# A two-layer decoder trunk on one Trainium2 core: an up tile cast and the first output rows moved to GpSimd, filler products on TensorE, and three casts and sums in another order

## What is computed

```
def rms_norm(x, w):
    y = xf * lax.rsqrt(jnp.mean(xf * xf, axis=-1, keepdims=True) + EPS)
    return (y * w).astype(x.dtype)
def swiglu(h, w_gate, w_up, w_down):
    return (jax.nn.silu(h @ w_gate) * (h @ w_up)) @ w_down
...
for l in range(DEPTH):
    x = x + 0.5 * swiglu(rms_norm(x, ffn1_norm[l]), ffn1_w_gate[l], ffn1_w_up[l], ffn1_w_down[l])
    ...
    x = x + 0.5 * swiglu(rms_norm(x, ffn2_norm[l]), ffn2_w_gate[l], ffn2_w_up[l], ffn2_w_down[l])
return rms_norm(x, final_norm)
```

## Time and profile before

| | |
|---|---|
| median of 3 runs | 1041.63 us (1041.61 to 1042.81) |
| profiled execution, its own time | 1040.92 us |
| its span | 1039.1 us |
| mean granted TensorE clock | 0.997 |
| TensorE busy | 1024.7 us (99%) |
| VectorE, ScalarE, GpSimd busy | 741.5, 606.9, 212.3 us |

### The profile page before, as it was taken

One profiled execution on the slowest core, in us unless ns is written; L12 is line 12 of the kernel. 1 busy time (PEld: TensorE's weight loads), 2 busy tenths in 40 slices (PEclk: granted clock), 3 DMA queues, 4 the chain that ended last, 5 costly groups with the idle time before them and its releaser, 6 DMA issues.

```text
span 1039.1 us, 18922 instructions
## 1 busy us (share of the span) xinstructions
PE 1024.7 (99%) x6464; PEld 886.3 (85%) x6464; DVE 741.5 (71%) x1201; ACT 606.9 (58%) x1070; POOL 212.3 (20%) x253
## 2 busy tenths in 40 slices
PE   7999999999999999999999999999999999999997
PEld 6888888899987888888888888889989888888885
DVE  5777666799776766666686666668986876666665
ACT  6555555787555655555675555558774556555554
POOL 3755111100400221111122111110014003111111
PEclk9999999999999999999999999999999999999999
DMA  8866666585124576666647666665731238666661
GB/s 260 263 190 188 188 185 191 143 240 154 62 62 122 163 211 192 183 188 195 183 133 217 194 183 183 193 172 161 223 102 63 82 101 245 200 183 188 192 185 41
DMA packets 249882, 176.79 MB, mean 170 GB/s; under 512 B 5876, under 2 KB 235401, under 8 KB 249705
## 3 DMA queue, kind: packets, MB, share of 16 engines
q1 hardware_dynamic: 248800, 174.35, 56.7%
q0 software_dynamic: 400, 1.43, 0.4%
q10 hardware_dynamic: 632, 0.34, 0.1%
HBM read 175.05 MB, written 1.05 MB: 169 GB/s over the span
## 4 chain that ended last, share of the span: by engine, by line
PE 94%; DVE 2%; ACT 1%; POOL 1%; issue 1%; DVEq 0%; POOLq 0%; ACTq 0%
PE bank L737 29%; PE bank L740 15%; PE bank L721 13%; PE bank L722 13%; PE bank L723 13%; PE bank L746 1%; PE bank L781 1%; PE bank L1109 1%; PE bank L1122 1%; DVE xr L2044 1%; PE bank L1042 1%; PE bank L995 1%; DVE Wl L1828 0%; PE bank L788 0%; PE bank L1024 0%
## 5 line engine op out<-in xcount | busy, mean ns | idle before, releaser
L1828 DVE TENSOR_TENSOR Wl<-raw,Wh 128x1024 fp32r<-128x1024 f32 x324 | 417.9, 1298 | 78.7 <-ACT Wh L1374 78.6
L1374 ACT ACTIVATE Wh<-raw 128x1024 fp32r<-128x1024 f32 x324 | 331.7, 1054 | 82.8 <-PE bank L723 82.2
L737 PE MATMUL bank<-X,Wh 128*128 128x512 f32 x1344 | 336.8, 393 | 0.0
L737 PEld LDWEIGHTS bank<-X,Wh 128*128 128x128 f32 x1344 | 246.7, 188 | 49.0
L740 PEld LDWEIGHTS bank<-X,Wl 128*128 128x128 f32 x1344 | 182.8, 189 | 14.7 <-DVE Wl L1828 0.9
L616 POOL TENSOR_TENSOR gact<-gact,pooled 128x256 f32<-128x256 f32 x88 | 77.6, 882 | 569.5 <-DVE gact L1922 432.4
L740 PE MATMUL bank<-X,Wl 128*128 128x256 f32 x1344 | 187.4, 282 | 0.0
L721 PE MATMUL bank<-Wh,aH 128*128 128x512 f32 x336 | 132.8, 395 | 1.4 <-DVE aL L1943 1.3
L722 PE MATMUL bank<-Wl,aH 128*128 128x512 f32 x336 | 131.8, 392 | 0.0
L723 PE MATMUL bank<-Wh,aL 128*128 128x512 f32 x336 | 131.5, 392 | 0.0
L1480 ACT ACTIVATE dec<-bank 128x256 f32<-128x256 f32 x88 | 33.6, 382 | 125.0 <-PE bank L740 124.9
(11 more groups left out here) (308 smaller groups left out, 1290.2 us busy)
## 6 DMA issues: line engine op xcount, KB each, us to landing
raw<-in_ffn_w_gate SPq DMA_DIRECT2D x88, 512.0 KB, 4.0
raw<-in_ffn_w_up SPq DMA_DIRECT2D x88, 512.0 KB, 3.7
raw<-in_ffn_w_down SPq DMA_DIRECT2D x88, 512.0 KB, 4.4
raw<-in_w_in SPq DMA_DIRECT2D x48, 512.0 KB, 4.6
raw<-in_w_out SPq DMA_DIRECT2D x16, 512.0 KB, 3.3
cst<-in_consts POOLq DMA_DIRECT2D x1, 1200.0 KB, 8.4
xr<-in_x SPq DMA_DIRECT2D x2, 512.0 KB, 4.3
out_x<-big SPq DMA_DIRECT2D x3, 256.0 KB, 2.1
```

Source lines behind the costliest of these rows:

```text
L737: nc.tensor.matmul(b[:, :], piece(Wh, s)[:, k, :], X[:, k, :, :], start=k == 0, stop=False)
L1374: return nc.scalar.activation(Wh[:, s, 0:D_MODEL], raw[:, s, :], ACT.Copy).then_inc(hi_cast.sem, 1)
L1828: return nc.vector.tensor_tensor(Wl[:, s, 0:D_MODEL], raw[:, s, :], Wh[:, s, 0:D_MODEL].bitcast(F32), ALU.subtract).then_inc(lo_cast.sem, 1)
```

## The change

In the head GpSimd casts piece 1 (the up tile of tile 0) in place of ScalarE, which only passes the count on. TensorE multiplies the unit matrix five more times (`KEEP`) between its transposes and the first gate product. On ScalarE the cast of piece 4 moves behind the gate and up sums of tile 0. On VectorE the two `variance` sums stand ahead of the low cast of piece 1. In the tail GpSimd weighs token half 0 (two products of 128x512) and later scales it (two more), VectorE no longer weighs the second quarter of half 1 apart, and SyncE's order of output DMAs becomes (0,0), (0,1), (1,1).

```diff
+KEEP = 5
...
+            for b in range(2):
+                sp.wait_ge(out_pool.sem, 2 + b + 1)
+                sp.dma_start(out[0, 0:P, b * NW:(b + 1) * NW], big[:, 0, b * NW:(b + 1) * NW]).then_inc(out_written.sem, 16)
             sp.wait_ge(out_dve.sem, 1)
-            sp.dma_start(out[0, 0:P, 0:NW], big[:, 0, 0:NW]).then_inc(out_written.sem, 16)
-            sp.wait_ge(out_dve.sem, 2)
             sp.dma_start(out[0, P:SEQ, NW:], big[:, 1, NW:]).then_inc(out_written.sem, 16)
-            sp.wait_ge(out_dve.sem, 3)
-            sp.dma_start(out[0, 0:P, NW:], big[:, 0, NW:]).then_inc(out_written.sem, 16)
...
+            pool.wait_ge(landed[1].sem, 16)
+            nc.gpsimd.tensor_copy(Wh[:, 1, 0:D_MODEL], raw[:, 1, :]).then_inc(up_first.sem, 1)
             pool.wait_ge(*lo_cast.at(0, 2))
...
+            pool.wait_ge(norm_w_in.sem, 16)
+            for b in range(2):
+                o, r, w = row_half(b)      # big[:, 0, q], xr[:, 0, q], norm_w[:, q]
+                pool.wait_ge(*x_new.at(DEPTH, b + 1))
+                nc.gpsimd.tensor_tensor(o, r, w, ALU.mult).then_inc(out_pool.sem, 1)
+            pool.wait_ge(root_dve.sem, 1)
+            pool.wait_ge(out_pool.sem, 2)
+            for b in range(2):
+                o, r, w = row_half(b)
+                nc.gpsimd.tensor_scalar(o, o, stat[:, 0, 7:8], None, ALU.mult).then_inc(out_pool.sem, 1)
...
+            def keep_warm(n):
+                for _ in range(n):
+                    nc.tensor.matmul(bank[3][:, 0:2 * P], ident, cst[:, C_IDENT:C_FIRST], start=True, stop=True)
...
-                    for _ in range(WARM):
-                        nc.tensor.matmul(bank[7][:, 0:2 * P], ident, cst[:, C_IDENT:C_FIRST], start=True, stop=True)
+                    keep_warm(WARM)
                     for c, b in ROW_ORDER:
...
+                    keep_warm(KEEP)
                     first_pair(layer, f, None)
...
                 if first:
-                    hi_first(layer, 0, 1)
+                    act.wait_ge(up_first.sem, 1)
+                    act.wait_ge(*hi_cast.at(layer, 1))
+                    act.sem_inc(hi_cast.sem, 1)
...
                     hi_first(layer, 0, 3)
-                    hi_first(layer, 0, 4)
...
                 gate_low(layer, f, 0, 0)
                 up_low(layer, f, 0, 0)
+                if layer == 0 and f == 0:
+                    hi_first(layer, f, 4)
                 hi_first(layer, f, 2)
...
                     lo_piece(layer, 0, 0)
-                    lo_piece(layer, 1, 1)
                     for c in range(HALVES):
                         variance(layer, n, c)
+                    lo_piece(layer, 1, 1)
...
             last(1, 0)
             variance(DEPTH, 0, 0)
             dve.wait_ge(norm_w_in.sem, 16)
-            weigh(0)
+            dve.wait_ge(*x_new.at(DEPTH, 3))
+            nc.vector.tensor_tensor(big[:, 1, 0:NW], xr[:, 1, 0:NW], norm_w[:, 0:NW], ALU.mult).then_inc(weighed.sem, 1)
             last(1, 1)
             final_root(0)
-            weigh(1)
             variance(DEPTH, 0, 1)
-            finish_row(0)
             final_root(1)
-            dve.wait_ge(weighed.sem, 2)
-            nc.vector.tensor_scalar(big[:, 1, NW:], big[:, 1, NW:], stat[:, 1, 7:8], None, ALU.mult).then_inc(out_dve.sem, 1)
-            finish_row(1)
+            dve.wait_ge(*x_new.at(DEPTH, 4))
+            nc.vector.scalar_tensor_tensor(big[:, 1, NW:], xr[:, 1, NW:], stat[:, 1, 7:8], norm_w[:, NW:], ALU.mult,
+                                           ALU.mult).then_inc(out_dve.sem, 1)
```

More of the change, by code:

```diff
@@ L306, in build @@
         rows_in = signal("rows_in")
+        up_first = signal("up_first")
+        out_pool = signal("out_pool")
         small_in = signal("small_in")
@@ L692, in _, with row_half @@
                 ffn(layer, 1)
+            def row_half(b):
+                q = slice(b * NW, (b + 1) * NW)
+                return big[:, 0, q], xr[:, 0, q], norm_w[:, q]
+            pool.wait_ge(norm_w_in.sem, 16)
[8 more added lines that the diff above has]
+                nc.gpsimd.tensor_scalar(o, o, stat[:, 0, 7:8], None, ALU.mult).then_inc(out_pool.sem, 1)
         @block.tensor
@@ L2357, in _ @@
             last = update(DEPTH - 1, 2, 0.5, downs_done.at(DEPTH - 1, 2 * TILES))
[L2359 to L2363, removed]
             def final_root(c):
@@ L2369, in final_root @@
                 dve.wait_ge(root_dve.sem, c + 1)
[L2371 to L2375, removed]
             last(0, 0)
```

## The result

The changed kernel took 1044.34 us, the median of 20 executions (1043.24 to 1044.73); the kernel before took 1042.64 (20 executions on the same chip, 1041.42 to 1043.74). Ratio 1.0016 [1.0009, 1.0022]: 1.7 us more, small but outside the interval. I had 1041.4 with a range to 1043.4, and an effect of -0.2.

A forecast was written before the change was run, and what follows sets the result against it. GpSimd's DMA-issue queue bounds the head; behind TensorE's last product a mainly VectorE chain bounds the tail. Head -0.39 and tail +0.2 gave -0.2: 1041.63 - 0.2 = 1041.4 us, range 1040.2 to 1043.4.

The forecast's parts named there:

- A: The forecast itself: head and tail both near level, clock 1.00 behind the second wait, 1041.4 us; chance 0.42.
- B: Clock falls behind the longer wait before the first down product, in front of unbroken work: 1.57 us lost, 1043.0; chance 0.3.
- GpSimd's queue bounds the head: Head: GpSimd's unbroken DMA issues delay its scaling of tile 0, hence the first down product; issues shift by 0.25 us.
- the chain: Head, up to the first down product: scaling of tile 0 ends 0.39 us earlier, so 25.37 becomes 24.98.
- The filler: Head, TensorE: ten instructions in 2.3 us before the gate products; if the clock holds, wide products save 1.2 us.
- the second wait: Head, TensorE before the first down product of tile 0: grows to 1.95 us from 1.15, swallowing gains ahead of it.
- GpSimd's product holds VectorE's weighing: Tail: VectorE's weighing of (1,0) waits for GpSimd's second weighing, stretched to 1.5 us; the update behind it 0.8 late.
- GpSimd's two scalings of 0.64 each by the earlier trace: Tail: GpSimd scales token half 0 until 1034.85 us; if twice as long, the tail loses 0.7 more.
- the root's small step: Tail, VectorE: first step of the second root waits for GpSimd's scalings until 1034.85 us, 0.25 later.
- C: Tail: GpSimd doesn't hold VectorE, so the work taken off pays in full, 0.8 us earlier, 1040.4; chance 0.15.
- D: Head: the filler does not hold the clock, 0.50 again from 11.4 us; the wait covers it, 1041.4; chance 0.08.
- E: GpSimd's queue gets much faster, or the loops gain in some unseen way: under 1039.5 us; chance 0.05.

The follow-up runs named there:

- head_only: The changed kernel with the tail of the kernel before: 1042.86 us against 1042.64 for the kernel before, ratio 1.0002.
- head_pool: head_only with GpSimd's two scalings of tile 0 moved ahead of its DMA issues of gate columns and masks: 1039.46 us against 1042.26 for the kernel before.
- head_lowfirst: head_only with VectorE's low cast of piece 1 ahead of the two sums again: 1043.45 us against 1042.54 for the kernel before, ratio 1.0005.
- best: The changed kernel with GpSimd's tile 0 scalings ahead of its large DMA issues, and in the tail GpSimd weighing only quarter (0,0): 1038.90 us, ratio 0.9968 to before.
- best_keep0: best without the filler (KEEP = 0): 1039.91 us against 1042.36 for the kernel before, ratio 0.9975.
- tail_only: The kernel before with the change's tail alone: 1043.56 us against 1042.64 for the kernel before, ratio 1.0011.
- tail_weigh: tail_only with the two scalings of token half 0 given to VectorE, GpSimd keeping both weighings: 1042.65 us, ratio 1.0002 to the kernel before.
- tail_one: tail_only with GpSimd weighing only quarter (0,0); VectorE scales it and does (0,1) in one instruction: 1041.72 us, ratio 0.9996 to the kernel before.
- tail_order: tail_only with SyncE sending output (1,1) between (0,0) and (0,1), as before: 1043.37 us, ratio 1.0008 to the kernel before.
- before_fill: The kernel before with four unit products added right before the first down product of tile 0: 1042.25 us against 1042.36, ratio 1.0001.
- after_one: The changed kernel with tail_one's tail: 1042.61 us against 1042.54 for the kernel before, ratio 1.0003.
- head_keep0: head_only without the filler (KEEP = 0): 1042.87 us against 1042.64 for the kernel before, ratio 1.0003.

## Why the prediction was wrong

The mechanisms hold almost throughout; two sizes, the choice between A and B, and the base do not. The measured 1044.34 is 2.9 above the forecast. 1.0 is the base: the kernel before over 20 executions against the three I summed from. The other 1.9 is the effect, +1.7 in place of -0.2: 0.7 of it is the tail (+0.9 by the profiles, forecast +0.2), some 0.6 the head (+0.2 in head_only, forecast -0.39), and the rest has no place.

**Right.** GpSimd's queue bounds the head: with the scalings ahead of the issues of gate columns and masks the chain drops by 2.0 us (head_pool). Its nine issues shift with the low cast, and the scaling then takes 0.82. The chain shortens by 0.35 (forecast 0.39), and head_lowfirst shows the edit that does most of it (0.28). The cast takes 1.04 and is hidden. The filler takes 2.32 us (2.3). The sixteen gate and up products behind it take 4.67 in place of 5.92 (1.25; forecast 1.2), and the second wait swallows it; once that wait is gone it is worth some 0.7 to 1.0 us (best against best_keep0). The second wait is 2.04 (1.95). In the tail GpSimd's product holds VectorE's weighing, by 1.55 - 0.68 = 0.87 us (0.85).

**Wrong: the term "GpSimd's two scalings of 0.64 each by the earlier trace rows".** They take 1.57 each, above even my bound of twice 0.64 (for which I had added 0.7 to the tail; it came to 0.9). The row is an affine select, another instruction. The trace of before has rows of the same one that I passed over: a multiplication by a scalar of each partition (line 580), an addition of a fixed number (line 590), and a product and a sum in one instruction (line 596), in the timeline of GpSimd:
```profile
36.72 0.71 POOL L580 TENSOR_SCALAR qT<-cst,pos_f 128x64 f32<-128x64 f32 x1
...
43.98 0.85 POOL L590 TENSOR_SCALAR qT<-qT 128x256 f32<-128x256 f32 x1
...
59.64 0.40 POOL L596 TENSOR_SCALAR kT<-qT 128x256 f32<-128x256 f32 x1
```
The first is 64 columns in 0.71 us, more than the 0.64 for 512 that I used (it took 0.45 in the changed kernel's trace, so part of it may be a hold). The second is 256 columns in 0.85, with no scalar of a partition: twice that is 1.70, near the 1.57 measured. So the scalar of each partition need not be what makes it long. In all 18 traces the instructions of this kind on 256 columns take 0.84 us or more with one operation (lines 589, 590, 592, 607 of the kernel before) and 0.40 to 0.62 with two (lines 596, 597, 600, 604). The scaling of the tail has one. Whether the scaling would be as short in that form, or why it is, wasn't tried. The estimate by the page of the Trainium skill beside it (GPSIMD Engine Reference, Engine selection), 0.43 us, was further off; the measured 1.57 decides. The tail came to +0.9, not +0.2, in the profiles (8.17 to 9.07; +1.1 by tail_only's ratio). Without the two scalings it is +0.3 (tail_weigh, 8.46), so this term is 0.57 of the 0.7 that the tail was off.

**Wrong, with it: what those scalings hold.** I let them hold the root's small step by 0.25. It was not held (0.22), while the last product was: 1.18 in place of the 0.75 that it takes in tail_weigh and tail_one. With both, that product ends 0.3 later than forecast (1039.40; 1036.2 moved by the 2.90 of TensorE's last product is 1039.1). The path that I had end the kernel, this product and then at once its DMA, was wrong too: the DMA leaves 0.75 behind it, since SyncE first waits for GpSimd's second scaling. In the other order the same scaling holds the last DMA, and the end comes only 0.09 earlier (tail_order). The rule I took from the earlier trace rows, that whatever reads two operands from SBUF waits for GpSimd, is too wide: a product of GpSimd held the weighing, its scaling did not hold a step of one column.

**Wrong: the likeliest case at the second wait.** I took A (clock 1.00 behind it, 0.42) over B (0.30). The clock fell, at the place, for the length (3.4 us) and at the price (1.57; measured 1.6 from the first down product to the last) that B had. In the eight profiles of this document where it fell there, it made the stretch behind 1.4 to 2.1 us longer. But B explains the level more than the difference. I had read one execution of the kernel before, where the fall was hidden; in five of seven profiles with its head the fall is as open as in the changed kernel. Where an execution of before hides its early fall and one of the changed kernel does not, the 0.35 us of the chain is given back several times over. I take this for the reason that the head's shorter chain shows in no median (head_only is at +0.2 [-0.7, +1.1] us and not at -0.39); the interval holds both, so it isn't shown. The mean clocks point the same way (22 of 117 executions of before at 0.998, none of the changed kernel's 20).

**Rivals.** C is out: GpSimd holds VectorE, and tail_one gains exactly by getting out of its way. D did not occur: the clock held from 11 us to the second wait in all seven profiles with the filler. That the filler is what held it is likely and not certain, since it held there in six of the eleven profiles without it too. E did not occur with this change, though its first half, a GpSimd queue that delivers earlier, is what head_pool made.

**Left open.** What decides whether a wait of some 2 us is followed by the low clock (8 in 10 profiles). Why the first transposes are slow in some executions. Where the slower half of before_fill's executions loses its time. Whether the 0.4 us between the two halves alone (1.3) and the whole (1.7) is more than noise. And whether GpSimd's scaling in a form with two operations would have made the forecast's tail come true.

## What to carry to other kernels

Price an instruction from a row of the same instruction in the same form, not only of the same size and engine: GpSimd's scaling took 2.5 times as long as its affine select of 512 columns (1.57 against 0.64 us), and rows of its own kind, 0.85 for 256 columns, stood in the same trace. Before tuning what feeds a wait, look at what the releasing engine's queue is busy with: moving two small products ahead of DMA issues took 1.97 us off the chain, where the reordering of casts and sums had taken 0.33. And profile a kernel more than once before taking a stall or a clock from its trace: only one of 137 executions was faster than the one shown here, and it hid the event that five of seven profiles of the same head show.

## What the hardware showed that I had not expected

GpSimd's 128x512 multiplication by a scalar of each partition took 1.57 us, longer than its product of two tensors of the same size (1.27 to 1.30); of its 128x256 instructions of that kind, those with one operation took 0.84 us and more and those with two 0.40 to 0.62; its cast of 128x1024 to fp32r took 1.04, about VectorE's and ScalarE's time. Under GpSimd's scaling VectorE was held only in part: nothing on one column, 0.43 us on a product of 512 columns. TensorE's clock held or fell behind like waits (second wait: 2.04 us fell in the changed kernel, 2.03 held in after_one; first wait: 2.62 us fell in the kernel before, 2.62 held in head_keep0). One such fall, 3.4 us at 0.50, costs 1.4 to 2.1 us when work is unbroken behind it and nothing when a later wait takes it up (chain 15.64 us with an early fall, 15.65 without). The first transposes ran in 1.0 to 1.9 us for eight, and the first gate product, behind them, began between 9.71 and 10.98 us from one execution to the next.
